# Joined values in the dilated attention layer: v by token from two panels, the other 56 tiles in 14 panels

## What is computed

```python
q, k, v, z = split(h @ w_in, [3*1024, 2*3*1024, 7*1024])   # w_in: 1024 x 8192, 3 dilation rates, 8 heads of 128
q, k = rope(q), rope(k)
for g, r in enumerate((1, 4, 16)):        # windows 128, 512, 2048
    o_g, lse_g = banded_attention(strided(q_g, r), strided(k_g, r), strided(v, r))
o = sum(softmax(lse)_g * o_g)             # one softmax over the joined scores of the three rates
y = (o * silu(z)) @ w_out;  x = x + gate * y;  out = rms_norm(x) * final_g
```

## Time and profile before

| | us |
|---|---|
| median of 3 runs (1623.54 to 1627.70) | 1627.55 |
| the profiled execution | 1623.5 |
| its span | 1621.7 |
| TensorE busy in the span | 1405.4 (87%) |
| VectorE, ScalarE busy | 658.9, 482.8 |
| mean granted TensorE clock | 0.939 |

### The profile page before, as it was taken

The page is one execution under the profiler, slowest core; times in us unless marked ns, Lnnn a source line. Parts: engine busy times, 40 slices in busy tenths (PEclk is TensorE's granted clock), DMA queues, the critical chain, the costliest instruction groups (busy, mean ns, idle before and its releaser), DMA issues.

```text
span 1621.7 us, 17185 instructions
## 1 busy us (share of the span) xinstructions
PE 1405.4 (87%) x6530; PEld 946.7 (58%) x6530; DVE 658.9 (41%) x1144; ACT 482.8 (30%) x717; POOL 84.6 (5%) x139
## 2 busy tenths in 40 slices
PE   6999996997787779878739999989999999999976
PEld 5787774332222323322227888767788878878765
DVE  4567746010000000000065656545555654565545
ACT  6462431110000000100153222334444534544432
POOL 2010001110000000100021010000000000000000
PEclk9999996999889999988959999989999999999988
DMA  8737338999999999999774553221212122121001
GB/s 356 306 130 271 145 113 322 348 386 393 399 406 400 385 385 404 373 395 395 318 287 144 207 195 130 104 80 52 104 52 104 53 78 79 61 96 52 1 1 65
DMA packets 41004, 347.71 MB, mean 214 GB/s; under 512 B 6080, under 2 KB 6208, under 8 KB 22592
## 3 DMA queue, kind: packets, MB, share of 16 engines
q1 hardware_dynamic: 29632, 304.69, 48.3%
q0 software_dynamic: 10304, 38.84, 7.0%
q10 hardware_dynamic: 960, 2.70, 0.4%
HBM read 321.56 MB, written 24.64 MB: 213 GB/s over the span
## 4 chain that ended last, share of the span: by engine, by line
PE 48%; DVE 3%; ACT 2%; issue 2%; DMA 1%; DVEq 0%; POOL 0%; SPq 0%; ACTq 0%; POOLq 0%
PE ps L259 46%; PE ps L649 1%; ACT ar L798 1%; DVE b_NL L1242 0%; DVE ar L1234 0%; DMA ar<-y_scratch,rt 0%; PE ps L708 0%; DVE hres L1676 0%; ACT ar L811 0%; PE ps L265 0%; DVE hres L1669 0%; ACT b_NH L807 0%; DMA y_scratch<-ar 0%; DVE ar L1856 0%; ACT ar L1012 0%
## 5 line engine op out<-in xcount | busy, mean ns | idle before, releaser
L259 PE MATMUL ps<-ring,ar 128*64 128x512 f32 x720 | 266.8, 640 | 61.5 <-issue 49.2
L259 PE MATMUL ps<-ar 128*128 128x128 f32 (+6 forms) x1022 | 290.5, 439 | 12.8 <-DVE ar L1587 4.6
L259 PE MATMUL ps<-b_NH,b_WH 128*128 128x512 f32 x768 | 203.7, 401 | 9.3 <-ACT b_NH L807 4.2
L1617 DVE TENSOR_TENSOR ar<-ar,ps 128x256 f32<-128x256 f32 x34 | 14.3, 422 | 482.1 <-ACT ar L939 482.1
L259 PEld LDWEIGHTS ps<-ring,ar 128*64 128x64 f32 x720 | 78.3, 146 | 224.0 <-issue 206.2
L259 PE MATMUL ps<-b_NH,b_WL 128*128 128x512 f32 x768 | 197.4, 393 | 0.0
L259 PE MATMUL ps<-b_NL,b_WH 128*128 128x512 f32 x768 | 190.4, 391 | 0.0
L1175 DVE TENSOR_TENSOR b_WL<-ring,b_WH 128x1024 fp32r<-128x1024 f32 x112 | 136.7, 1221 | 99.5 <-ACT b_WH L750 99.5
L259 PEld LDWEIGHTS ps<-b_NH,b_WH 128*128 128x128 f32 x768 | 142.1, 190 | 40.7 <-ACT b_NH L807 8.9
L259 PEld LDWEIGHTS ps<-b_NH,b_WL 128*128 128x128 f32 x768 | 145.9, 190 | 30.6
L259 PEld LDWEIGHTS ps<-b_NL,b_WH 128*128 128x128 f32 x768 | 144.9, 189 | 30.2
(11 more groups left out here) (260 smaller groups left out, 1550.7 us busy)
## 6 DMA issues: line engine op xcount, KB each, us to landing
ring<-in_wts_dram SPq DMA_DIRECT2D x79, 2048.0 KB, 17.4
spare<-in_wts_dram SPq DMA_DIRECT2D x31, 2048.0 KB, 37.4
ar<-in_wts_dram SPq DMA_DIRECT2D x22, 2048.0 KB, 39.7
ring<-in_wmod_dram SPq DMA_DIRECT2D x24, 512.0 KB, 5.0
ar<-in_wmod_dram POOLq DMA_DIRECT2D x24, 512.0 KB, 4.2
y_scratch<-gate POOLq DMA_DIRECT2D x11, 1024.0 KB, 21.1
y_scratch<-ar SPq DMA_DIRECT2D x68, 128.0 KB, 31.7
hres<-in_x_dram SPq DMA_DIRECT2D x4, 512.0 KB, 5.9
```

The costliest lines, as they stand in the source:

```text
L259: return pe.matmul(o, l, m, start=start, stop=stop, skip_group_check=True)
L1617: return dve.tensor_tensor(hh[s], sg[s], ps[:, b, 256:512], ALU.mult)
```

## The change

The v columns of all heads leave the tiles and become two panels by token, P_V and P_V + 1, right behind the first panel. Their eight banks are copied into `vall`, which takes over one of the four ring slots; from P_DIL on, panels go through the three others. The 56 tiles that are left fill 14 panels in the order q0, q1, q2, k0, k1, k2, z of each head, but z of heads 6 and 7 come as the last two tiles. They use banks 0, 1 and 5 in turn, and wait for the tile three before. The transposes of v, the semaphores vc and vt and the buffers `vk` are gone. Attention is placed by `step_behind`: step 0 of a head is behind its z tile, steps 1 to 5 behind tiles 0 to 4 of the next head, and nothing is behind tile 5; for head 6 step 0 is behind the first tile of head 7, and head 7 has steps 0 and 1 behind the last two tiles. Four steps are left behind the last tile.

```diff
+P_V = P_DIL + 1
+FEAT = {*range(0, 2), *range(P_C0, P_CO), P_DIL, *range(P_V + 2, P_DO)}
-        for i in range(P_C0, N_PANELS):
+        for i in range(P_C0, P_DIL):
             settle(i, free_ring[(i - P_C0) % RING])
+        for i in range(P_DIL, N_PANELS):
+            settle(i, free_ring[(2, 3, 0)[(i - P_DIL) % 3]])
-        vk = [area(7168 + 512 * j, 4, 128) for j in range(2)]
+        vall = ring[:, free_ring[1], :].rearrange("p (t e) -> p t e", t=4)
+        TILES = [(h, r) for h in range(8) for r in range(7) if h < 6 or r < 6] + [(6, 6), (7, 6)]
+        PROJ = (0, 1, 5)
+        def step_behind(g):
+            h, r = TILES[g]
+            if g == 54:
+                return 7, 0
+            if g == 55:
+                return 7, 1
+            if r == 6:
+                return h, 0
+            if h == 7:
+                return 6, r
+            return h - 1, r + 1
```

On the tensor engine:

```diff
-            for h in range(8):
-                i = P_DIL + 2 * h
...
-                        for q in range(4):
-                            t = pe.transpose(ps[:, 5, q * 128:(q + 1) * 128], sw[(7 * h + 6) % 2][:, q * 128:(q + 1) * 128],
-                                             ident[:, :])
-                        t.then_inc(S["vt"], 1)
...
+            def first(j):
+                if j == 3:
+                    proj_free(0)
+            def behind(g):
+                if g >= 7:
+                    proj_free(g - 3)
+            b4 = tuple(PROJ[g % 3] for g in range(4))
+            lead_panel(P_DIL, op_b, N_DL, b4)
+            run(feature_tiles(P_DIL, op_b, b4, (2, 3), first))
+            token_panel(P_V, op_b, (2, 3, 4, 6))
+            proj_free(3)
+            pe.wait_ge(S["vk"], 2)
+            token_panel(P_V + 1, op_b, (7, 0, 2, 3))
+            proj_free(1)
+            proj_free(2)
+            for q in range(1, 14):
+                i = P_V + 1 + q
+                b4 = tuple(PROJ[(4 * q + j) % 3] for j in range(4))
+                for j in feature_tiles(i, op_b, b4, range(4), lambda j, q=q: behind(4 * q + j)):
+                    h, step = step_behind(4 * q + j)
+                    if h >= 0 and step < 6:
+                        attention(h, step)
+            for step in range(2, 6):
                 attention(7, step)
```

On the scalar engine:

```diff
+            def silu_z(g):
+                h = TILES[g][0]
+                if h >= 2:
+                    act.wait_ge(S["y"], 8 + h - 1)
+                evict(tile_panel(g), g % 4, zT[h % 2], ACT.Silu, "z", PROJ[g % 3])
+            for c in range(2):
+                for n in range(4):
+                    next_hi(P_V + c, n)
+                for t in range(4):
+                    evict(P_V + c, t, vall[:, t, c * 512:(c + 1) * 512], ACT.Copy, "vk",
+                          ((2, 3, 4, 6), (7, 0, 2, 3))[c][t])
+            for g in range(4, 56):
+                next_hi(tile_panel(g), g % 4)
+                if TILES[g][1] < 6:
+                    rope(g)
+                else:
+                    silu_z(g)
+                h, step = step_behind(g)
+                if h >= 0 and step < 6:
+                    attention(h, step)
```

On the vector engine the order is the same, with the gate of head 6 behind the softmax of step 0 of head 7:

```diff
+                if h >= 0 and step < 6 and (h, step) != (6, 5):
+                    attention(h, step)
+                if g == 54:
+                    gated_values(6)
```

On the sync engine:

```diff
-            for i in range(P_C0 + 1, P_DIL + 4):
+            for i in range(P_C0 + 1, P_DIL + 3):
                 load(i)
...
-            for i in range(P_DIL + 4, N_PANELS):
+            for i in range(P_DIL + 3, N_PANELS):
                 load(i)
```

More of the change, by code:

```diff
@@ L38 @@
 cc tt0 xr cv y zc tm
-sw ra rb qk z vc vt vk scr att fl pt av
+sw ra rb qk z vk scr att fl pt av
 """.split()
-FEAT = {*range(0, 2), *range(P_C0, P_CO), *range(P_DIL, P_DO)}
+P_V = P_DIL + 1
+FEAT = {*range(0, 2), *range(P_C0, P_CO), P_DIL, *range(P_V + 2, P_DO)}
 ORDER = {6: (2, 3, 0, 1), 7: (2, 3, 0, 1)}
@@ L246, in program, with tile_panel @@
         T_IN, T_RT, T_CV, T_DL = 0, 8, 16, 24
-        TOKENS = [2, 3, 4, 5, 6, 7, P_CO, P_CO + 1, P_DO, P_DO + 1]
+        TOKENS = [2, 3, 4, 5, 6, 7, P_CO, P_CO + 1, P_V, P_V + 1, P_DO, P_DO + 1]
+        TILES = [(h, r) for h in range(8) for r in range(7) if h < 6 or r < 6] + [(6, 6), (7, 6)]
+        PROJ = (0, 1, 5)
+        def tile_panel(g):
+            return P_DIL if g < 4 else P_V + 1 + g // 4
+        def step_behind(g):
[9 more added lines that the diff above has]
+            return h - 1, r + 1
         def tile_done(i, j):
@@ L311, in token_panel @@
                 NH, NL, WH, WL = ops
+                bank = b if isinstance(b, tuple) else (b, b + 1, b + 2, b + 3)
                 for n, ch in enumerate(ORDER.get(i, (0, 1, 2, 3))):
@@ L321, in token_panel @@
                             for kk in range(2):
-                                k, o = 2 * ch + kk, ps[:, b + t, :]
+                                k, o = 2 * ch + kk, ps[:, bank[t], :]
                                 nh, nl = (a[:, k, t * 128:(t + 1) * 128] for a in (NH, NL))
@@ L333, in token_panel @@
                         for t in range(4):
-                            mm(ps[:, b + t, :], NH[:, k, t * 128:(t + 1) * 128], h[:, kk, :], n == 0 and kk == 0, False)
+                            mm(ps[:, bank[t], :], NH[:, k, t * 128:(t + 1) * 128], h[:, kk, :], n == 0 and kk == 0, False)
                     pe.wait_ge(S["lo"], c + 1)
@@ L659, in values @@
                 for q in range(4):
-                    t = mm(ps[:, ob, p * 128:(p + 1) * 128], vk[h % 2][:, q, :], PT[:, q * 128:(q + 1) * 128],
+                    t = mm(ps[:, ob, p * 128:(p + 1) * 128], vall[:, q, h * 128:(h + 1) * 128], PT[:, q * 128:(q + 1) * 128],
                            q == 0, q == 3)
@@ L713, in tensor_program @@
-            for step in range(6):
+                h, r = TILES[g]
+                if r == 6:
+                    pe.wait_ge(S["z"], h + 1)
+                else:
+                    pe.wait_ge(S["ra"], 6 * h + r + 1)
+            def first(j):
+                if j == 3:
+                    proj_free(0)
[4 more added lines that the diff above has]
+            lead_panel(P_DIL, op_b, N_DL, b4)
@@ L1118, in attention @@
                     exp_scores(h, step)
[L1120 to L1150, removed]
@@ L1151, in scalar_program @@
-            for step in range(6):
+            for g in range(4):
+                if g < 2:
+                    hi(P_DIL, g + 2)
+                elif g == 3:
+                    hi(P_V, 0)
+                rope(g)
[5 more added lines that the diff above has]
+                          ((2, 3, 4, 6), (7, 0, 2, 3))[c][t])
@@ L1152, in scalar_program @@
+            for g in range(4, 56):
+                next_hi(tile_panel(g), g % 4)
+                if TILES[g][1] < 6:
+                    rope(g)
+                else:
+                    silu_z(g)
+                h, step = step_behind(g)
+                if h >= 0 and step < 6:
+                    attention(h, step)
+            for step in range(2, 6):
                 attention(7, step)
-            act.wait_ge(S["wdone"], done(cno(P_DIL + 15, 3)))
+            act.wait_ge(S["wdone"], done(cno(P_DO - 1, 3)))
@@ L1778, in vector_program, with rope @@
             dve.wait_ge(S["rope"], 32)
-            def rope(h, i, j, r):
-                m, w, o = 6 * h + r, sw[(7 * h + r) % 2], ps[:, j % 2, :]
+            def rope(g):
+                h, r = TILES[g]
+                m = 6 * h + r
+                w, o = sw[m % 2], ps[:, PROJ[g % 3], :]
                 q = qkd[h % 2][:, r, :]
@@ L1817, in attention, with gated_values @@
                 if step == 5:
[L1818 to L1842, removed]
+                    gated_values(h)
+            def gated_values(h):
+                dve.wait_ge(S["av"], 4 * h + 4)
+                dve.wait_ge(S["z"], h + 1)
+                dve.tensor_tensor(yTd[:, h, :], ps[:, 6 + h % 2, :], zT[h % 2], ALU.mult).then_inc(S["y"], 1)
+            for g in range(4):
+                if g < 2:
+                    lo(P_DIL, g + 2)
+                elif g == 3:
+                    lo(P_V, 0)
+                rope(g)
+            for c in range(2):
+                for n in range(4):
+                    next_lo(P_V + c, n)
+            for g in range(4, 56):
+                next_lo(tile_panel(g), g % 4)
+                if TILES[g][1] < 6:
+                    rope(g)
+                h, step = step_behind(g)
+                if h >= 0 and step < 6 and (h, step) != (6, 5):
+                    attention(h, step)
+                if g == 54:
+                    gated_values(6)
+            for step in range(2, 6):
                 attention(7, step)
@@ L2129, in lay_out @@
     dl = feat(w["dil_w_in_2"][0])
-    for h in range(8):
-        for q in ([0, 1024, 2048, 7168], [3072, 4096, 5120, 6144]):
-            wp.append(np.concatenate([dl[:, :, a + 128 * h:a + 128 * h + 128] for a in q], axis=2).reshape(128, 4096))
+    off = [0, 1024, 2048, 3072, 4096, 5120, 7168]
```

(4 more changed lines are left out.)

54 lines of the change are left out of this document (13 added, 41 removed).

## The result

The changed kernel took a median of 1607.35 us (1606.90 to 1607.69, four runs) against 1626.01 us; the ratio is 0.9886, 95% interval 0.9869 to 0.9903. The prediction was 14.1 us less than before and a median of 1613.4; the first comparison gave 18.7 us less, and its median lies 0.35 us above the lower end of the stated range (1607 to 1620). Two later comparisons of the same kernel gave 0.9907 (0.9889 to 0.9925) and 0.9900 (0.9882 to 0.9918), 13.2 and 15.8 us less. The profiled execution took 1606.9 us (foreseen: 1609.4), its span 1605.2.

The account below looks back on a forecast made before the run. TensorE was taken as the bound. 9.24 (turn of v) + 1.45 (three banks) - 1.23 (scores(0) moved into the loop) + 4.6 (tail) = 14.1 us less: profiled execution 1609.4, median 1613.4, range 1607 to 1620.

Parts of the forecast that it names:

- What bounds: Middle of the layer: TensorE, busy 98.5 of 100 us, sets the time; other engines count only where it waits.
- The turn of v: Loop, heads 0 to 6: wait for the copy and four transposes, 1.32 us each, go; 9.24 us less.
- By token at the same price: The two v panels: v's matmuls stay 192 in number and cost the same by token; taken as 0.
- Three banks: First panel: the third tile goes to bank 5 and waits for nothing, 1.45 us less; nothing in the loop.
- The three shorter waits: Loop: scores(h, 0), flip(0) and flip(1) still wait nowhere, with slack of 1.9, 2.1 and 0.96 us; cost 0.
- the last key: Rival at scores(h, 0): the last key's rope or z tile is late, 1.32 us in 7 heads, 1622.6; chance 6%.
- VectorE as the bound: Rival in the softmax slots: VectorE's work grows and flips wait; at 1.8 us growth +12.8 us, 1640; chance 3%.
- a late panel: Rival at the ring of three: one load lands 22 us later than the median does, 1630; chance 2%.
- The table loads: ScalarE behind z tiles: 1.28 us each without a drain; rival of 2.56 us each gives 1618.3, chance 3%.
- The tail: Last tile's end to scores(2): 7.7 us instead of 12.36, so 4.6 us less; bounds 3.3 and 6.0.
- its clock term: Tail, values and flip before scores(2): run at the 1.2 GHz level again, adding 1.37 us to 6.35.
- Sum: Whole kernel: 14.1 us less, the profiled execution at 1609.4 and the median at 1613.4.

Follow-up runs that it names:

- e6: The kernel before with only the transposes of v left out, v entering the products unturned; median 1613.51 us, ratio 0.9920.
- e1: The changed kernel with its tiles in two PSUM banks (0 and 1) instead of three; median 1612.13 us, ratio 0.9912.
- e3: The changed kernel with ten matmuls, results unread, ahead of waits in the tail to keep TensorE busy; median 1605.45 us, ratio 0.9874.
- e8: The kernel before with eleven matmuls, results unread, keeping TensorE busy in the tail; median 1620.73 us, ratio 0.9962.
- e4: The changed kernel with two banks and the old order of tiles and steps, leaving only v by token; median 1619.38 us, ratio 0.9960.

## Why the prediction was right, step by step

- **What bounds.** TensorE, and nothing else up to T: in the changed kernel it is busy 100.00 us of 100, and no wait stands between 1108 us and T. Shown. The period of a head is 48.84 us (scores(0) from 1177.95 to 1470.99, six heads), for 49.0 foreseen.
- **The turn of v.** Foreseen 9.24 us in the loop for 7 turns of 1.32. In e6, which takes away nothing else, 10.18. The term was 10% small: the first eight matmuls behind a turn began a new group and took 1.94 us to the next start instead of 1.81 (1201.29 to 1203.23 in the trace of before), 0.13 each, which the prediction put at nothing by leaving it out.
- **By token at the same price.** Shown: passes of v begin 1.81 us apart, and both panels run without a gap.
- **Three banks.** Foreseen 1.45; 1.45 in the first panel between the traces (5.08 against 3.63), and 1.58 from L to T in e1, again with the 0.13 behind it. These eight times 0.13 are the 1.0 us by which L to T fell more (10.47) than foreseen (9.46).
- **The three shorter waits.** None appeared, and neither did the rivals that lived on them (the last key, VectorE as the bound, a late panel). The table loads took 1.28 us each, and the activation began 1.29 us behind the start of each (1521.41 to 1522.70, 1523.32 to 1524.61). The Trainium skill's "ScalarE: Activation LUTs", section "What ACT_TABLE_LOAD costs", adds a drain to the load. This trace does not agree.
- **The tail.** Foreseen: 7.7 us from T to scores(2), for 12.36 before, and 6.35 at full clock. Read: 6.71 in the first trace, 7.80 in e1, 6.50 in e3. At full clock, before (e8: 1542.76 to 1553.83, 11.07) to after (6.50) is 4.57, and the sum without its clock term gives 10.99 - 6.35 = 4.64. So the work and the waits were right, and the clock was not. The prediction let it cost both tails the same. Against full clock it cost the kernel before 4.13 us from T to E (71.97 to e8's 67.84) and the changed kernel 5.55 (68.79 to e3's 63.24), 1.42 more: values(0) ran mostly at the upper level, but from scores(2) to P it took 17.47 us, for 13.35 at full clock, where the kernel before took 14.90. So T to E lost 3.2 us and not 4.6. "The same work and the same waits" from scores(2) on was true; the same clock was not. Why the clock fell there in three executions of the changed kernel and elsewhere in e1 is open.
- **Sum.** 14.1 predicted; 13.7 between the two traces, 15.0 at full clock, 13.2 and 15.8 in the two later comparisons. That 13.7 lies so near is partly luck: the prediction had 1.0 us too little up to T and 1.4 too much behind it. The 18.7 of the first comparison is 5 us more. That its few runs all had an early start of the layer I can show for the profiled ones (L 2.8 us earlier, where the prediction wanted the stretch before 1104 us the same), not for the rest. The forecast of the profiled execution, 1609.4, stands 2.5 us above 1606.9: these 2.8, less the 0.4 of the sum. The two later medians, 1612.64 and 1610.20, lie nearer to the forecast of 1613.4. What moves L is only located: between two of ScalarE's roundings that enclose the experts' stage lie 575 to 581 us in these traces, and the first of them begins between 231 and 237 us; behind the second, L still varies by 3 us. Its cause was not tried.

## What to carry to other kernels

When one engine is busy without a gap, the gaps and instructions removed add up to the gain: here 9.5 us for 10.5, and to 0.1 us once the 0.13 of each fresh start is counted. Each wait that a new order shortens can be checked beforehand by laying the producer's chain beside the time at which the consumer wants its result. An instruction that goes may have been the cover of something else: with v taken out of the last slot and no z moved into it (e4), only 3.5 of the 13.7 us are left in the traces, though 1.6 of what is missing is the third bank. And a tail full of short waits can cost more than the waits: ten matmuls whose results nobody reads raised the granted clock there from 0.77 to 1.00 and brought 5.5 us.

## What I had not expected

A group of matmuls behind transposes, float32 products or a wait needs 0.10 to 0.13 us more for its first eight than one that goes on. The tail's clock loss is not fixed by the order of the work: T to P was 24.2 us in three executions of the changed kernel and 22.59 in the one of e1, whose code differs there only in the banks of the last tiles. Whether a second execution of e1 would repeat its time was not tried. And single executions of one kernel lie up to 7.8 us apart for the changed kernel and 11.0 for the kernel before (1621.22 to 1632.23), more than any single term of this change but the turn. In the three traces of the changed kernel the stages ahead of this layer make 6.1 us of it.
